# A two-block hybrid layer stack in split fp32 on one core: a third weight piece converted ahead, the gates' logarithms placed ahead of the attention steps, and query sums placed ahead of rotations

## The chip, the cores and the metric

One Trainium2 chip, of which one core runs the kernel. The time is device time of one execution in microseconds; the time stated is the median of several. The engines are called PE (TensorE, matmuls), PEld (its weight loads), ACT (ScalarE), DVE (VectorE), POOL (GpSimd) and SP (SyncE, which issues the DMAs). The granted clock is the share of full speed (2.4 GHz) that PE was given in a stretch.

## What is computed

A sequence of 16 meta and 512 other tokens of width 1024, in fp32, goes through two layers of a first block and two of a second. A layer of block 1 (`hybrid_layer`) is:

```python
h = rms_norm(x, norm_g);  z = h @ w_in
aq, ak, av, ag, mq, mk, mv, mi, mf, mo, mgate = jnp.split(z, split_points(), axis=-1)
q = apply_partial_rope(rms_norm(aq, q_norm_g), cos, sin)      # 16 heads of 64, 2 kv heads
k = apply_partial_rope(rms_norm(ak, k_norm_g), cos, sin)
ya = sliding_window_sink_attention(q, k, v, sink) * silu(ag)
mq, mk = split(silu(causal_depthwise_conv(concat[mq, mk])))
log_i = mi + b_i;  log_f = log_sigmoid(mf + b_f)              # the gates, one row per head
hm = mlstm_chunkwise(mq, mk, mv, log_i, log_f)
ym = rms_norm(hm) * sigmoid(mo) * silu(mgate)
return x + concat([ya, ym]) @ w_out
```

A layer of block 2 has a memory of keys and values, made by a projection of a normalised memory, differential attention in 32 steps, three groups of local attention, softmaxes over dilated units, gates, three branches and an output projection. All of it is again projections of the normalised input by slices of one wide weight matrix, with softmaxes and gates on the results.

## The kernel before, in words

**Weights.** All weights come as a stream of pieces of 128 x 1024 fp32 values (512 KB) in a fixed order. A step `("w", r)` turns piece r from the staging ring (2 buffers, `st`) into two halves: ACT copies it to a rounded high half `ch`, DVE subtracts that from the piece and gives the low half `cl`. Both have rings of 3 buffers (`NST, NCV = 2, 3`). The wait of ACT ahead of the copy is for the DMA of piece r and for the last matmul that read piece r-3. SP issues the DMA of piece r+2 once `cl` of piece r is done. Activations are kept as `hh` and `hl`, so each product takes three matmuls: hh x ch, hl x ch, hh x cl. A projection of one 128-wide tile over 8 slices of K and 2 token halves in block 1 is 48 matmuls; a unit of two tiles reads two pieces, and each piece serves both tiles with half of K.

**Order.** The class `Order` writes one list of steps by hand, and each engine executes its share of each step in the order of the list, with semaphore waits where a step needs the result of another engine. So what stands ahead of a step in the list stands ahead of it in the queue of every engine that both use. `Order.weights` puts the next `("w", r)`; `proj` and `projr` call it twice behind a unit's last tile, and in the places where a piece serves one tile alone (`lvpm`, `o1`, `br`, `o2`) it is called once for each piece. At the start of the list, `order()` puts the first two pieces at k = 4 and 6 of the loop over the input tiles. The evacuation of a projection (`cvev`, `qkev`, `agev`, `lvev`, `lgev`, `gtev`, `dqkev`) is put behind `proj`, so behind those conversions.

**Block 1, attention stage (`block1`).** 32 attention steps: `sA` (transposes, scores, maximum), `sB` (exponentials), `sC` (probabilities times values), for step s, s-1, s-2 in loop turn s, over head pairs; beside each, `fill(s)` puts projections by the table `SCHED1`: mv tiles (`mvmm`) in steps -3 to 1, conv tiles 0 and 1 at steps 2 and 3, query tiles 2 and 3 at steps 4 and 5, mv again at 6 to 10, and so on in turns of 8 steps; from 29 the attention gate's tiles (`ag`). Attention steps 8, 16 and 24 are the first to use query tiles 2, 4 and 6. For a query tile, `chain()` walks through three stages, one per loop turn: x = 0 `qsum` (sums of squares on PE, DVE scale, pow on POOL), x = 1 `rope` (scaled tile times cosine on POOL, shifted copy by DMA times sine and an addition on DVE), x = 2 `ropeq` (writes the `ZR` query operand on DVE). Query tiles come in pairs one step apart, so while the odd tile is at stage x, the even one is at x + 1; `st["turn"]` holds them in order of the tile.

**Gates in block 1.** `gra` takes bias, absolute value, exponential and logarithm on a 4 x 528 tile (ACT); the exponential and the logarithm are in different table sets, so it has two table loads. `grf` has 8 parts: 0 and 1 are additions, a fill and scans on DVE, the next ones smaller, part 7 writes and reads rows through DMAs. `grt` brings results to token order. In the kernel before `gra` is put at step 0 behind `sA`, `grf` parts 0 to 7 at steps 1 to 8 and `grt` at step 5.

**Block 2 (`block2`).** 35 steps of differential attention with projections beside them (`SCHED2`), `dnorm`, three local groups (`lq`, then values by `lvmm`/`lvpm` with `lvev`, then scores and softmax `lS`), the softmax over 3 parts (`lse0`, `lse1`, `lse2`) between projections `mq(0)` and `mq(1)`, 16 transposed dilated units (`eT`, `eP`) with the gates `lg` ahead and behind, the additions `yasp`, memory attention `fA`/`fB` with gate projections (`mg`, `gate`), branches `br` and the output `o2`.

In the profile all engine calls of a kind have one line, that of the helper: L92 matmul, L95 transpose, L98 activation, L101 tensor_tensor, L105 tensor_scalar, L109 scalar_tensor_tensor, L116 scan, L119 copy, L122 reduce.

Of the kernel before, what the change touches and what calls it, by code (L numbers as in the profile page):

```python
# [290 lines left out]
class Order:  # L291
# [6 lines left out]
    def put(self, *step):  # L298
        self.o.append(step)
# [90 lines left out]
    def block1(self, l, sums):  # L390
        put, nid = self.put, l
# [3 lines left out]
        def later():  # L395
            if st["conv"]:
                t, g = st["conv"]
                put("conv", l, t, g, self.nsq())
            st["conv"] = None

        def chain():

            todo, st["turn"] = st["turn"], []
            for t, n, x in todo:
                if t == 8 and x == 0:
                    put("qkn", l)
                    n = rot(t)
                else:
                    put(("qsum", "rope", "ropeq")[x], l, t, n)
                if x < (1 if t == 8 else 2):  # L410
                    st["turn"].append((t, n, x + 1))

        def rot(t):
            put("rot", l, t, self.rot)
            self.rot += 1
            return self.rot - 1

        def qk(t, u):
            self.proj(("q", l, t), nid, L, u, t % 2)
            chain()  # L420
            put("qkev", l, t)
            st["turn"].append((t, rot(t), 0))

        def fill(s):
            later()
            for kind, a, b in SCHED1[s]:
                if kind == "mv":
                    if b == 0:
                        st["u"] = self.unit(1, l, 3328 + 256 * a)
                    put("mvmm", l, a, b, st["u"])  # L430
                    if b == 4:
                        self.weights()
                        self.weights()
                    put("mvev", l, a, b)
                    continue
                later()
                if a % 2 == 0:
                    st["u"] = self.unit(1, l, {"cv": 2304, "ag": 1280, "q": 0}[kind] + 128 * a)
                if kind == "q":
                    qk(a, st["u"])  # L440
                    continue
                self.proj((kind, l, a), nid, L, st["u"], a % 2)
                if kind == "cv":
                    g = self.ng()
                    put("cvev", l, a, g)
                    st["conv"] = (a, g)
                else:
                    n = self.nsq()
                    put("agev", l, a, n, self.ng())
# [12 lines left out]
        g = self.ng()  # L462
        put("vev", l, g)
        chain()
        self.norms(nid, 3, 4)
        put("gr", l)
# [8 lines left out]
        put("mvones", l)  # L475
        for a in range(3):
            fill(a - 3)
            chain()
        for s in range(35):
            if s < 32:  # L480
                put("sA", l, s)
            if s == 0:
                put("gra", l)
            if 1 <= s < 9:
                put("grf", l, s - 1)
            if s == 5:
                put("grt", l)
            if not any(x[0] == "q" for x in SCHED1[s]):
                chain()
            fill(s)  # L490
            if 0 <= s - 1 < 32:
                put("sB", l, s - 1)
            if 0 <= s - 2 < 32:
                put("sC", l, s - 2)
            if s == 26:
                put("m_s", l)
            if s == 27:
                put("m_t", l)
            if s == 28:
                put("m_o", l)  # L500
            later()
# [297 lines left out]
def order():  # L799
    m = Order()  # L800
    m.put("load")
    m.put("lines")
    m.put("consts")
    add, flush = m.squares(0)
    for k in range(9):
        if k < 8:
            m.put("xt", k)
        if k:
            m.put("raw", 0, k - 1)
        if k in (4, 6):  # L810
            m.weights()

    def first(k):
        add(k)
        if k == 7:
            flush()
    sums = m.block1(0, first)
    m.block1(1, sums)
    for l in range(2):
        m.block2(l)  # L820
    assert m.taken == len(m.plan) == m.converted
    return m.o
def program(nc, I, out):
    with ExitStack() as ctx:
        sig = Signals()
        steps = order()

        def sb(name, cols, dt=F32, p=128):
# [2095 lines left out]
```

How the kernel before makes its waits and increments, by code:

```python
    def wait_ge(self, *keys):  # L77
        for k in keys:
            if self.e is None:
                self.sig.asked.add(k)
            elif self.sig.at[k] is not None:
                name, v = self.sig.at[k]
                if v > self.seen.get(name, 0):
                    self.e.wait_ge(self.sig.sem[name], v)
                    self.seen[name] = v
# [954 lines left out]
            def acquire(key, ring, apart=False):  # L1040
                n = turn_of.get(ring, 0)
                turn_of[ring] = n + 1
                banks = rings[ring][n % len(rings[ring])]
                for b in banks:
                    pe.wait_ge(*held[b])
                    held[b] = [("free", key, b - banks[0])] if apart else [("free", key)]
                held_by[key] = banks
# [6 lines left out]
            def xt(k):  # L1055
                acquire(("xt", k), "PA")
                ps = ps2(("xt", k))
                pe.wait_ge(("x",))
                for a in range(4):
                    pe.transpose(ps[:, 0, 128 * a:128 * a + 128], xs[:, a, 128 * k:128 * k + 128], idf)
                pe.transpose(ps[:, 1, 0:16], meta[:, 128 * k:128 * k + 128], cst[0:16, C_ID:C_ID + 16]).then_inc(
                    "pe_x", ("full", ("xt", k)))
# [1 line left out]
            def sqp(sid, k, n):  # L1064
# [2 lines left out]
                    acquire(key, "P3")  # L1067
                ps = ps2(key)
                pe.wait_ge(("sqa", sid, k), ("ones",))
                for j, (o, w) in enumerate([(0, HALF), (HALF, HALF)] if lo == 0 else [(0, 512)]):
```

## Time and profile before

| | us |
|---|---|
| median of 3 runs | 3089.79 |
| lowest to highest | 3086.59 to 3089.86 |
| profiled execution | 3090.76 |
| its span | 3088.9 |
| PE busy | 2958.4 |
| DVE busy | 1617.1 |
| ACT busy | 1264.7 |
| POOL busy | 181.9 |
| mean granted clock | 0.981 |

Busy is the time in which an engine has an instruction under way. The page also lists groups of instructions with the idle time of the engine just before them and what ended it; the timeline gives each instruction with its start and, in brackets, the idle time before it and the engine and tile whose result ended it. "x2" is two like instructions run together, and the duration is that of both.

### The profile page before, as it was taken

Reading aid. Unit: us, or ns where it says so; the run is one execution under the profiler, and the core shown is the slowest. Engines: PE = TensorE matmul, PEld = TensorE weight load, DVE = VectorE, ACT = ScalarE, POOL = GpSimd, SP = SyncE. Lnnn points to the kernel's source line nnn. Section 1 sums busy time; section 2 is a strip of 40 time slices with the busy share of each in tenths; the row PEclk is TensorE's granted clock in tenths of the full one; section 3 lists DMA queues with packets and bytes.
Section 4 is the critical chain, followed back from the end, with each engine's and each line's share of the span. In section 5 each row is a group of like instructions: output and inputs, shape, how many; then the busy total and the mean of one; then the engine's idle time right before and its main releaser. Section 6 shows DMA issues by size and latency. Waiting matters only on the chain.

```text
span 3088.9 us, 44910 instructions
## 1 busy us (share of the span) xinstructions
PE 2958.4 (96%) x18366; PEld 2582.2 (84%) x18366; DVE 1617.1 (52%) x3255; ACT 1264.7 (41%) x2640; POOL 181.9 (6%) x207
## 2 busy tenths in 40 slices
PE   8899999988999999999999999999999999999998
PEld 6799888987999889888888877887888888877886
DVE  5666645346675453677433564334677433554324
ACT  4455423244554232565424433223566334433222
POOL 2100000010000000100000000000100000000000
PEclk9899999998999999999999999999999999999999
DMA  3111321211113222322233222333322232222222
GB/s 102 55 44 58 105 67 62 86 48 44 57 57 105 67 80 85 113 86 68 82 110 96 69 82 69 96 96 96 113 87 68 82 117 89 81 70 76 95 96 82
DMA packets 99735, 250.24 MB, mean 81 GB/s; under 512 B 8597, under 2 KB 44845, under 8 KB 99274
## 3 DMA queue, kind: packets, MB, share of 16 engines
q1 hardware_dynamic: 99530, 247.37, 25.2%
q8 instruction: 145, 2.38, 0.3%
q14 instruction: 60, 0.49, 0.0%
HBM read 239.60 MB, written 6.50 MB: 80 GB/s over the span
## 4 chain that ended last, share of the span: by engine, by line
PE 81%; DVE 11%; ACT 4%; issue 1%; DMA 1%; POOL 1%; DVEq 0%; POOLq 0%; SPq 0%; ACTq 0%
PE ps L92 78%; PE ps L95 3%; ACT Z L98 2%; DVE cl L101 2%; DVE Z L101 2%; DVE Z L109 1%; DVE ZR L101 1%; DVE Z L119 1%; DMA st<-in_stream_dram 1%; DVE Z L105 1%; DVE stat L122 1%; ACT ch L98 1%; ACT L98 0%; POOL stat L101 0%; DVE sq L109 0%
## 5 line engine op out<-in xcount | busy, mean ns | idle before, releaser
L92 PE MATMUL ps<-hh,ch 128*128 128x264 f32 (+1 forms) x2688 | 824.6, 348 | 54.2 <-DVE cl L101 32.1
L92 PE MATMUL ps<-hl,ch 128*128 128x264 f32 (+1 forms) x2880 | 851.7, 340 | 0.0
L92 PE MATMUL ps<-hh,cl 128*128 128x264 f32 (+1 forms) x2688 | 811.7, 343 | 0.0
L101 DVE TENSOR_TENSOR cl<-st,ch 128x1024 fp32r<-128x1024 f32 (+1 forms) x436 | 495.8, 1152 | 531.3 <-ACT ch L98 531.1
L92 PEld LDWEIGHTS ps<-hh,ch 128*128 128x128 f32 x2688 | 468.4, 192 | 128.7 <-issue 27.4
L98 ACT ACTIVATE ch<-st 128x1024 fp32r<-128x1024 f32 (+1 forms) x436 | 424.8, 990 | 357.0 <-PE ps L92 328.3
L92 PEld LDWEIGHTS ps<-hl,ch 128*128 128x128 f32 x2880 | 500.1, 192 | 59.1
L92 PEld LDWEIGHTS ps<-hh,cl 128*128 128x128 f32 x2688 | 468.4, 191 | 58.9
L98 ACT ACTIVATE Z<-ps 128x512 f32<-128x512 f32 (+7 forms) x510 | 218.9, 438 | 600.3 <-PE ps L92 479.8
L92 PE MATMUL ps<-ZR,ch 128*128 128x264 f32 (+2 forms) x1728 | 426.5, 342 | 5.6 <-DVE cl L101 5.2
L92 PEld LDWEIGHTS ps<-ZR,ch 128*128 128x128 f32 x1728 | 289.1, 191 | 48.8 <-issue 12.9
L92 PE MATMUL ps<-Z 128*128 128x128 f32 (+11 forms) x1564 | 272.7, 318 | 25.2 <-DVE Z L119 15.1
L92 PEld LDWEIGHTS ps<-Z 128*128 128x128 f32 (+6 forms) x1564 | 205.8, 186 | 81.5 <-issue 47.3
L92 PE MATMUL ps<-ZR,cl 128*128 128x512 f32 (+2 forms) x704 | 223.7, 348 | 0.0
L92 PE MATMUL ps<-ch,hh 128*128 128x256 f32 (+2 forms) x736 | 214.2, 291 | 2.5 <-DVE cl L101 2.5
L92 PE MATMUL ps<-cl,hh 128*128 128x256 f32 (+2 forms) x736 | 211.2, 287 | 0.0
L92 PE MATMUL ps<-ch,hl 128*128 128x256 f32 (+2 forms) x736 | 210.7, 286 | 0.0
L98 ACT ACTIVATE Z<-Z,stat 128x512 f32<-128x512 f32 (+4 forms) x264 | 151.2, 587 | 121.3 <-DVE stat L105 112.4
L92 PE MATMUL ps<-ZR 128*128 128x256 f32 (+4 forms) x1040 | 179.0, 333 | 9.9 <-DVE stat L105 9.9
L95 PE MATMUL ps<-cst,Z 128*128 128x128 f32 (+3 forms) x974 | 151.0, 274 | 8.0 <-DVE Z L101 5.9
L119 DVE COPY Z<-ps 128x512 f32<-128x512 f32 (+7 forms) x132 | 70.5, 547 | 157.5 <-PE ps L92 115.6
L92 PEld LDWEIGHTS ps<-ZR 128*128 128x128 f32 (+2 forms) x1040 | 123.4, 191 | 29.8 <-DVE stat L105 11.3
(133 smaller groups left out, 3213.6 us busy)
## 6 DMA issues: line engine op xcount, KB each, us to landing
st<-in_stream_dram SPq DMA_DIRECT2D x372, 512.0 KB, 3.6
st<-in_stream_dram SPq DMA_DIRECT2D x64, 256.0 KB, 3.3
Z<-decay_rows SPq DMA_DIRECT2D x8, 904.0 KB, 6.4
Z<-bias_lines SPq DMA_DIRECT2D x16, 448.0 KB, 4.1
ya_spill<-Z SPq DMA_DIRECT2D x8, 512.0 KB, 4.5
Z<-ya_spill SPq DMA_DIRECT2D x2, 2048.0 KB, 7.7
Z<-in_x_dram SPq DMA_DIRECT2D x4, 512.0 KB, 5.6
Z<-in_mem_dram SPq DMA_DIRECT2D x2, 1024.0 KB, 6.1
```

Of the source, the lines that this page charges most:

```text
L92: return Ins(self, self.e and self.e.matmul(o, a, b, start=start, stop=stop, skip_group_check=True))
L95: return Ins(self, self.e and self.e.transpose(o, a, i))
L98: return Ins(self, self.e and self.e.activation(o, i, f, **kw))
L101: return Ins(self, self.e and self.e.tensor_tensor(o, a, b, op))
L105: return Ins(self, self.e and self.e.tensor_scalar(o, a, s1, s2, op0))
L109: return Ins(self, self.e and self.e.scalar_tensor_tensor(out=o, in0=a, scalar=s, in1=b, op0=op0, op1=op1))
L119: return Ins(self, self.e and self.e.tensor_copy(o, i))
L122: return Ins(self, self.e and self.e.tensor_reduce(o, i, X, op, negate=negate))
```

## The change

Three edits, all of them to the order of the steps: (1) at the start a third piece is converted ahead, so that each later conversion step converts the piece one further in the stream; (2) `gra` goes from step 0 to the prologue turn a = 0, ahead of `chain()`, `grf` parts 0 and 1 to a = 1 and 2, parts 2 to 7 to steps 1 to 6, and `grt` to step 3; (3) within `chain()` the tiles are taken in order of their stage instead of order of the tile, so the odd tile's sum comes ahead of the even tile's rotation, and the odd tile's rotation ahead of the even tile's `ropeq`.

```diff
@@ -401,7 +401,7 @@
         def chain():
 
             todo, st["turn"] = st["turn"], []
-            for t, n, x in todo:
+            for t, n, x in sorted(todo, key=lambda y: y[2]):
                 if t == 8 and x == 0:
                     put("qkn", l)
                     n = rot(t)
@@ -475,15 +475,17 @@
         put("mvones", l)
         for a in range(3):
             fill(a - 3)
+            if a == 0:
+                put("gra", l)
+            else:
+                put("grf", l, a - 1)
             chain()
         for s in range(35):
             if s < 32:
                 put("sA", l, s)
-            if s == 0:
-                put("gra", l)
-            if 1 <= s < 9:
-                put("grf", l, s - 1)
-            if s == 5:
+            if 1 <= s < 7:
+                put("grf", l, s + 1)
+            if s == 3:
                 put("grt", l)
             if not any(x[0] == "q" for x in SCHED1[s]):
                 chain()
@@ -807,7 +809,7 @@
             m.put("xt", k)
         if k:
             m.put("raw", 0, k - 1)
-        if k in (4, 6):
+        if k in (4, 6, 8):
             m.weights()
 
     def first(k):
```

## Rows read from the trace of the kernel before

**Rows 1.** the page: busy time of the engines, its share of the span, instructions

```profile
PE 2958.4 (96%) x18366; PEld 2582.2 (84%) x18366; DVE 1617.1 (52%) x3255; ACT 1264.7 (41%) x2640; POOL 181.9 (6%) x207
```

**Rows 2.** waits of PE: line, releaser: us in total, times, longest

```profile
PE ps L92 <- DVE cl L101: 45.2, 27, 6.9
```

**Rows 3.** timeline, PE, steps 2 to 7: start, us, instruction, [idle before <-releaser]

```profile
101.99 0.78 PE L92 MATMUL ps<-hh,ch 128*128 128x264 f32 x2 [6.86 <-DVE cl L101]
123.95 0.78 PE L92 MATMUL ps<-hh,ch 128*128 128x264 f32 x2 [3.64 <-DVE cl L101]
151.42 0.58 PE L92 MATMUL ps<-ZR 80*128 80x256 f32 x1 [2.41 <-DVE stat L105]
```

**Rows 4.** windows: stretch, length, busy per engine, PEclk, DMA share, GB/s

```profile
102.00:106.50 4.50, 4.50 (x20) 4.50 (x21) 3.16 (x10) 1.32 (x5) 0.00 (x0) 0.50 0.67 221
107.00:110.00 3.00, 3.00 (x27) 3.00 (x26) 2.04 (x3) 0.00 (x0) 0.00 (x0) 1.00 0.00 1
536.00:540.00 4.00, 3.28 (x15) 3.31 (x16) 3.66 (x8) 2.24 (x3) 0.00 (x0) 0.61 0.40 131
```

**Rows 5.** timeline, ACT, step 0 (`gra`)

```profile
89.84 0.72 ACT L98 ACTIVATE Z<-Z,par 4x528 f32<-4x528 f32 x1
90.59 1.32 ACT L98 ACTIVATE Z<-Z 4x528 f32<-4x528 f32 x2
91.93 1.28 ACT L98 ACT_TABLE_LOAD   x1
93.22 0.64 ACT L98 ACTIVATE Z<-Z 4x528 f32<-4x528 f32 x1
```

**Rows 6.** timeline, DVE, steps 1 and 2: scan and subtractions

```profile
99.48 1.25 DVE L116 TENSOR_TENSOR_SCAN Z<-Z 4x528 f32<-4x528 f32 x1
100.66 2.32 DVE L101 TENSOR_TENSOR cl<-st,ch 128x1024 fp32r<-128x1024 f32 x2
```

**Rows 7.** timeline, POOL, DVE and PE, steps 14 to 16: tiles 4 and 5

```profile
206.50 1.95 POOL L101 TENSOR_TENSOR stat<-stat,par 128x10 f32<-128x10 f32 x1 [51.83 <-ACT Z L98]
...
208.41 1.30 POOL L101 TENSOR_TENSOR Z<-Z,cst 128x528 f32<-128x528 f32 x1
...
216.59 1.04 DVE L109 SCALAR_TENSOR_TENSOR stat<-stat,par 128x1 f32<-128x1 f32 x2
...
220.70 0.71 DVE L101 TENSOR_TENSOR ZR<-Z,ZR 128x528 fp32r<-128x528 f32 x1
221.32 0.70 DVE L101 TENSOR_TENSOR rot<-rot,cst 128x528 f32<-128x528 f32 x1
...
221.51 0.28 PE L92 MATMUL ps<-mskb,idb 128*128 128x144 bf16 x2 [1.19 <-issue]
```

**Rows 8.** timeline, PE, start of the output projection of block 1

```profile
536.72 1.10 PE L92 MATMUL ps<-ZR,ch 128*128 128x264 f32 x4 [1.78 <-DVE cl L101]
```

**Rows 9.** timeline, PE, block 2: memory's k/v; start of layer 1

```profile
1252.15 0.39 PE L92 MATMUL ps<-ch,ZR 128*128 128x256 f32 x1 [1.78 <-DVE cl L101]
...
2199.73 0.47 PE L92 MATMUL ps<-hh,ch 128*128 128x512 f32 x1 [2.25 <-DVE cl L101]
```

**Rows 10.** timeline, local values of group 2 and scores behind them

```profile
1738.63 1.06 ACT L98 ACTIVATE ch<-st 128x1024 fp32r<-128x1024 f32 x1 [5.21 <-PE ps L92]
...
1739.73 1.23 DVE L101 TENSOR_TENSOR cl<-st,ch 128x1024 fp32r<-128x1024 f32 x1 [5.05 <-ACT ch L98]
...
1741.48 1.29 DVE L119 COPY Z<-ps 128x512 f32<-128x512 f32 x2 [0.53 <-PE ps L92]
...
1743.66 2.20 PE L92 MATMUL ps<-Z 128*128 128x128 f32 x16 [0.50 <-DVE stat L112]
```

**Rows 11.** timeline, `yasp` additions behind the second gate unit, and PE

```profile
1830.31 3.09 DVE L101 TENSOR_TENSOR ZR<-Z,ZR 128x512 fp32r<-128x512 f32 x5
...
1836.55 0.50 PE L92 MATMUL ps<-hh,ch 128*128 128x512 f32 x1 [1.43 <-ACT Z L98]
```

**Rows 12.** timeline, PE, behind gate tile (0,1)

```profile
1882.35 2.47 PE L92 MATMUL ps<-Z 128*128 128x128 f32 x10 [3.07 <-DVE Z L119]
```

## Prediction

> **What bounds the kernel now.** I read the page's table of engines first [rows 1]: TensorE (PE) is busy 2958.4 of a span of 3088.9 us, so 130 us is all that any reordering can give back, apart from the clock; VectorE, ScalarE and GpSimd have most of their time free. So this is a case of waits, not of work. The waits of PE come next [rows 2]: the largest single item is the low half of a converted weight piece (`cl`), 45.2 us in 27 waits. I then listed each matmul that had been waited for, in order of time. Two waits of each block-1 layer make up most of it, 6.86 and 3.64 us [rows 3], with twins 601 us later; both layers together 21.0 us. Their neighbours are a wait for statistics, 2.41 us, ahead of an attention step [rows 3]. What is left of the 45.2: 1.25 x2 at the k/v unit, 1.78 x2 in the output projection [rows 8], 0.32 x4, and so 16.9 us for block 2, of which [rows 9] are two of the three longest. What a wait costs beyond itself is in the windows [rows 4]: behind the 6.86 us idle, the granted clock is 0.50 (1.2 of 2.4 GHz) for 4.5 us and back at 1.00 after; half of full speed over 3.5 to 4.5 us is some 1.7 to 2.2 us of lost matmul time. The window behind the 1.78 us of the output projection shows 0.61. I count 1.7 us for a wait like these that appears or goes.
>
> **How the three edits work.** *Third piece.* A unit has two halves of weights; with three converted buffers the conversion put at a unit's end was that of the piece whose buffer the unit's first half had freed. Now the last one put is that of the piece whose buffer frees at the end of the unit's last matmul. Gain: the first piece of the next unit is ready a unit earlier, so most `cl` waits can go. Cost: ScalarE (ACT) stands in the conversion's wait until the projection ends, then converts for 1.06 us [rows 10]; the evacuation of that projection's PSUM, put behind it, starts 1.1 us later; VectorE (DVE) stands in its subtraction (1.16 us each, [rows 6]) until ACT is done, so what DVE does with the unit's result starts 2.3 us after the projection's end, and SyncE's issue of the next piece stands in the same line. Where the result isn't needed soon this is hidden by the matmuls behind it; where PE's next work needs it, it is paid. Bytes, matmuls and conversions stay the same in number.
>
> *Gates' logarithms.* In ACT's queue at step 0 lie 0.72 + 1.32 + 1.28 (table load) + 0.64 us [rows 5], and a second load of 1.28 before the next Exp, 5.2 us in all, ahead of the pieces' conversion; on DVE the scan's 1.25 us, and an addition and a fill before it, lie ahead of the two subtractions (2.32 us, ending at 102.98), and PE's 6.86 us end there, at 101.99 [rows 3, 6]. Moved to the three prologue steps, where PE has mv matmuls whose weights are there, this goes from the path. The load itself lasts 1.28 us and the rows on both sides touch it (90.59 + 1.32 = 91.91, load at 91.93, next row at 93.22), so two switches take 2.6 us. The Trainium skill, "ScalarE: Activation LUTs", section What ACT_TABLE_LOAD costs, puts a load with the drain before it at some 2.7 us, so two at 5.3: by the page the move would free 2.7 us more of ACT, and the trace does not agree, since no drain stands between the rows.
>
> *Query sums ahead of rotations.* Sorting by stage turns "rotate the even tile, sum the odd one" into the reverse, and one step later puts the odd tile's rotation ahead of the even tile's last step, which writes the ZR that the attention step sA(8, 16, 24) multiplies.
>
> **Block 1, per layer, term by term** (+ is time saved).
> Steps -3 to 8: the 6.86 us lose ACT's 5.2 us; the conversion is also a unit ahead, so the wait goes nearly whole, but sA(0) and the tiles behind it are then late by the gates' work placed in the prologue; followed through, PE's gain at the first conv unit is about 4. The 3.64 us end on a DVE that had the next part of the gates' scan, as long as the one in [rows 6] or more, ahead of two subtractions; they shrink, and then the chain sum, pow, rotation, last step of tiles 2 and 3 sets sA(8) as it does now (it is what the 2.41 us of [rows 3] and its neighbours belong to). I get sA(8) 4.1 us earlier, after a wait of its own of over 1 us that costs 1.7 of clock: +2.4. Bounds: the two waits whole with clock, 6.86 + 3.64 + 2 x 1.7 = +13.9; or the chain eats it all, 0 (not below: no ACT or DVE work is added there). I take 2.4 since the chain's steps are the same instructions as before on both engines.
> sA(16): now the last step for tile 4 ends at 220.70 + 0.71 and PE goes on at 221.51 after 1.19 us idle (the profile names "issue", but the start stands at the end of that DVE row) [rows 7]. Sorted, tile 5's add pair (0.70 + 0.71, starting at 221.32 before) lies ahead: 1.4 us; and tile 4's rotation itself waits for a pow of 1.95 us on GpSimd that was behind the 1.30 us product [rows 7], of which about 0.6 reaches the path: -2.0, and the longer idle, about 3.2 us, turns the clock down: -1.7. Sum -3.7. sA(24) the same with less to wait for: -1.8 - 1.7 = -3.5. Bounds of each: 0 (if the even rotation's neighbours free DVE earlier) to -5.
> On GpSimd beside DVE: the pair of small DVE operations at 216.59 lasts 1.04 us in [rows 7], while GpSimd runs its product. The Trainium skill, "SBUF — State Buffer", section Who interferes with whom, gives this for a DVE instruction with two SBUF inputs beside a GpSimd one that reads SBUF. By it the sort, which moves the pow up by a step, moves such a meeting rather than adding one: 0.7 us either way, no more than the bounds just named.
> The output projection's 1.78 us [rows 8] goes, with the slow clock behind it (0.61 in [rows 4]): +3.4. Bounds 0 and 3.4. The 0.32 x2: +0.6. The attention gate unit that closes the stage pays the late evacuation: -1.1 - 0.4 = -1.5 (bounds 0 and -2.8).
> Sum: 2.4 - 3.7 - 3.5 + 3.4 + 0.6 - 1.5 = -2.3, for two layers -4.6.
>
> **Block 2.** *Gains.* Of the 16.9 us of `cl` waits, those in the memory's k/v (the first row of [rows 9]) end on a DVE that does norms ahead of the subtraction: the lead saves a third, 1.1 + 1.5. The waits at the block's start (0.88 and, behind a late piece, 2.25, the second row of [rows 9]) and ahead of dnorm (1.18 x2) go; the one behind the second softmax piece goes but its subtraction then lies ahead of the softmax's normalisation, -0.5 net in one layer and 0 in the other; 0.4 x2 goes. Sum 2.6 + 3.1 + 2.4 - 0.5 + 0.8 = +8.4. Bounds: 0 and 16.9.
> *Losses, per layer.* Local values (lvpm, then lS): now the projection ends at 1741.38, DVE copies at 1741.48 (1.29 us), and PE has 16 matmuls of its own and waits 0.50 us for the scores [rows 10]. The conversion at 1738.63 waited for the other half's end, [5.21 <-PE]; the new one waits for 1741.38, 1.06 us of ACT and 1.23 us of DVE come ahead of the copy, so it starts at 1743.7 instead of 1741.5: -2.25. This is for groups 1 and 2; for group 0, where two subtractions lie near there already, -1.3: -5.8. First gate unit ahead of the exponentials' transposes: -1.8 (of 2.3, 0.5 is idle). Second: the five additions (3.09 us), the maximum and the exponentials behind them already make PE wait 1.43 us [rows 11], so all that is put ahead on DVE and ACT, 1.9 us, is paid. Gate tile (0,1): PE already waits 3.07 us for a copy behind three additions [rows 12]: two conversions lie ahead now and one more of them moves behind the end: -1.35. First attention step of a head pair, three times: -0.4 each, -1.2. Sum -12.05, for two layers -24. Bounds: half of it, if PE's matmuls in flight cover as in the other units, -12; or with the clock: four of these waits grow over 1 us, 8 x 1.7 = -13.6 more, -38. I take -24 without clock, since two of the four are over 1 us today and pay for the clock already.
>
> **Sum.** -4.6 + 8.4 - 24 = -20. The profiled execution took 3090.76 us, 1.0 above the median of 3089.8; on the median 3089.8 + 20 = 3110.
>
> **Rivals.**
> A. *The lead pays and the queueing is covered.* If PE has work everywhere behind a unit's end (it is 96% busy and matmuls are queued ahead), the block-2 losses are nothing and the sort costs little: +8.4, and block 1 +2.4 + 3.4 + 0.6 without the sort's 7.2, up to +13.9 in the first term: 2 x 6.4 to 2 x 17.9. Time 3089.8 - 8.4 - 12.8 = 3068.6, at the far end 3046. For it: 45.2 us are named by the profile. Against: [rows 10, 11, 12] show PE idle just behind a unit's end already. It decides if the copy after a local-values unit starts less than 0.5 us late.
> B. *Waits are exchanged.* Same edits, half of block 2's losses (-12), gains +8.4 and block 1 even: 3089.8 + 3.6 = 3093, within the noise of the rest.
> C. *Clock on top.* As forecast, with new idle of over 1 us behind local values and gates turning the clock down each time: 3110 + 13.6 = 3124. It decides if the new idle stretches are followed by a clock as that of [rows 4].
> D. *The third piece changes nothing.* The ring has three buffers and the wait for the buffer is the same instruction order; if no conversion starts earlier than now because the staging DMA behind it is late, only sort and gates act: -3.7 - 3.5 + 2.4 per layer, 3089.8 + 9.6 = 3099. Against: [5.21 <-PE] in [rows 10] shows the buffer, not the DMA, as the last thing waited for.
>
> **How the numbers follow.** Forecast 0.35, C 0.18, D 0.07, A 0.22, B 0.18. Likeliest 3110 (its own range 3099 to 3118). For 8 in 10 the range leaves out A's far half and C's end: 3068 to 3126. Less than 0.2% (6 us) can't be told from no change: faster 0.22 (A, the better edge of B), same 0.14 (most of B), slower 0.64 (forecast, C, D, the rest of B).
>
> **What would show it.** Right: behind a unit's last matmul in block 2 the ACT row is a conversion of 1.06 us that waited for PE, and the copy starts over 2 us after the projection's end; PE's waits for `cl` fall from 45.2 to under 20, those for DVE Z, stat and ACT Z grow by over 25; idle ahead of sA(16) is about 3 us; 6.86 is gone, the clock behind it 1.00; the output projection has no wait. Wrong: PE's idle at the local scores is still 0.5; sA(16) starts no later than its neighbour tiles before; or the prologue's steps show new waits of over 2 us (the gates' work ahead of sA(0)), which no term here contains.

## The result and the profile after

The changed kernel takes 3160.18 us (median of 4 runs, 3157.14 to 3164.36) against 3089.82 us of the kernel before in the same session: a ratio of 1.0238, interval 1.0225 to 1.0251. The medians are 70 us apart (the ratio gives 73). The direction was forecast; the size was not (+20), and the time lies above the range, which ended at 3126.

The page after, with the line that answers to [rows 1], and the chain of work that ended last:

```profile
span 3157.5 us, 45008 instructions
PE 2973.8 (94%) x18366; PEld 2592.1 (82%) x18366; DVE 1624.5 (51%) x3255; ACT 1264.9 (40%) x2640; POOL 184.8 (6%) x207
PE 77%; DVE 12%; ACT 5%; issue 3%; POOL 1%; DMA 1%; DVEq 0%; SPq 0%; POOLq 0%; ACTq 0%
```

The third line is the chain; before, it was PE 81%, DVE 11%, ACT 4%, issue 1%. The span grew by 68.6 us. The matmuls are the same in number (18366); PE is busy 15.4 us longer with them, which is the clock (mean 0.976, before 0.981), and so idle 53 us more. Split where block 2 begins, PE's busy time fell by 1.4 us ahead of it and grew by 16.8 us in it (1769.3 to 1786.1). The waits of PE (engine, line, releaser: us in total, times, longest), against the 45.2 us of [rows 2]:

```profile
PE ps L92 <- DVE ZR L101: 32.8, 14, 4.9
PE ps L92 <- ACT Z L98: 19.7, 12, 5.2
PE ps L92 <- DVE Z L109: 19.5, 15, 3.3
PE ps L92 <- DVE Z L119: 18.6, 16, 4.1
PE ps L92 <- DVE stat L112: 13.4, 8, 3.0
...
PE ps L92 <- DVE cl L101: 5.0, 5, 2.0
```

The waits for `cl` did what was forecast: 45.2 to 5.0 us. What took their place is larger: the query operand (ZR), evacuations by ACT (Z), gates' and branches' results (Z L109), local scores' statistics (L112). Where these lie is read by taking each matmul of the order in both traces and subtracting its start times (PE's order is the same but for ten small transposes of `grt` in each layer of block 1). The difference is -1.0 us when block 1 begins, +11.5 in its first layer's output projection, +24.1 in the second's, +48.6 at the end of block 2's first layer and +68.5 at the end. So block 1 lost 25 us (forecast 4.6) and block 2, with the end of block 1's last output projection, 44 (forecast 15.6).

The traced execution of the kernel before took 3090.76 us, and its medians in the sessions of the experiments are 3086 to 3088. So start times measured against it show a loss up to 5 us too small, a gain up to 5 us too large.

The attention step 16, which answers to [rows 7] (timeline; start, duration, instruction, idle before):

```profile
211.06 0.70 DVE L101 TENSOR_TENSOR rot<-rot,cst 128x528 f32<-128x528 f32 x1
211.23 2.34 POOL L101 TENSOR_TENSOR stat<-stat,par 128x10 f32<-128x10 f32 x1 [2.80 <-DVE stat L105]
213.54 2.60 POOL L101 TENSOR_TENSOR Z<-Z,cst 128x528 f32<-128x528 f32 x2
214.97 1.74 DVE L101 TENSOR_TENSOR Z<-Z,rot 128x528 f32<-128x528 f32 x1 [3.20 <-POOL Z L101]
216.63 0.68 DVE L101 TENSOR_TENSOR ZR<-ps,ZR 128x512 fp32r<-128x512 f32 x1
217.37 0.31 PE L95 MATMUL ps<-cst,ZR 128*80 128x128 f32 x1 [1.32 <-DVE ZR L101]
...
221.11 0.70 DVE L101 TENSOR_TENSOR rot<-rot,cst 128x528 f32<-128x528 f32 x1
221.85 0.71 DVE L101 TENSOR_TENSOR Z<-Z,rot 128x528 f32<-128x528 f32 x1
222.47 0.17 DVE L119 COPY Z<-Z 128x16 f32<-128x16 f32 x1
222.75 0.71 DVE L101 TENSOR_TENSOR ZR<-Z,ZR 128x528 fp32r<-128x528 f32 x1
223.56 0.28 PE L92 MATMUL ps<-mskb,idb 128*128 128x144 bf16 x2 [4.51 <-issue]
```

This is the sort at work. The odd tile's pow (2.34 us) now stands ahead of the even tile's cosine product on POOL, and DVE, which has begun that tile's rotation, stands 3.20 us for it with everything behind it: the operand made from PSUM (216.63), for which PE waits 1.32 us, the next softmax, tile 5's rotation, and last the operand of tile 4 (222.75), for which PE is idle 4.51 us instead of 1.19 (the profile says "issue", but PE starts 0.1 us behind the end of that DVE row). The addition itself takes 1.74 us with POOL's second product beside it. Before, it took 0.71:

```profile
213.39 0.71 DVE L101 TENSOR_TENSOR Z<-Z,rot 128x528 f32<-128x528 f32 x1
```

Windows behind two long idle stretches, one of 5.16 us ahead of 120.08 (for an evacuation) and this one of 4.51 us. The columns are stretch, length, busy of PE, PEld, DVE, ACT, POOL, clock, DMA share, GB/s:

```profile
120.10:124.50 4.40, 4.40 (x20) 4.40 (x21) 3.78 (x5) 1.92 (x6) 0.00 (x0) 0.50 0.66 232
223.60:228.00 4.40, 4.40 (x27) 4.15 (x28) 2.71 (x12) 1.64 (x6) 0.00 (x0) 0.61 0.00 0
```

Local values in block 2, which answer to [rows 10]:

```profile
1773.17 1.95 PE L92 MATMUL ps<-Z 128*128 128x128 f32 x16
1773.43 1.06 ACT L98 ACTIVATE ch<-st 128x1024 fp32r<-128x1024 f32 x1 [1.78 <-PE ps L92]
1774.39 1.07 ACT L98 ACTIVATE Z<-ps 128x512 f32<-128x512 f32 x2
1774.52 1.23 DVE L101 TENSOR_TENSOR cl<-st,ch 128x1024 fp32r<-128x1024 f32 x1 [1.61 <-ACT ch L98]
1775.66 1.28 DVE L119 COPY Z<-ps 128x512 f32<-128x512 f32 x2
...
1777.84 0.38 PE L92 MATMUL ps<-Z 128*128 128x128 f32 x1 [2.72 <-DVE stat L112]
```

As forecast, the conversion waits for the projection's end and DVE's copy starts 2.2 us later behind it; PE's idle went from 0.50 to 2.72.

### The profile page after: what moved, and what is told of

It is laid out like the page before. It is cut to its first block, busy times and chain, and to the rows that moved or that the text cites. A ratio compares the mean times of both kernels' runs of the same rounds, so it can differ in the third digit from the quotient of the medians.

```text
span 3157.5 us, 45008 instructions
## 1 busy us (share of the span) xinstructions
PE 2973.8 (94%) x18366; PEld 2592.1 (82%) x18366; DVE 1624.5 (51%) x3255; ACT 1264.9 (40%) x2640; POOL 184.8 (6%) x207
## 4 chain that ended last, share of the span: by engine, by line
PE 77%; DVE 12%; ACT 5%; issue 3%; POOL 1%; DMA 1%; DVEq 0%; SPq 0%; POOLq 0%; ACTq 0%
PE ps L92 74%; PE ps L95 3%; DVE cl L101 2%; ACT ch L98 2%; DVE Z L109 2%; ACT Z L98 2%; DVE Z L101 2%; DVE ZR L101 1%; DMA st<-in_stream_dram 1%; DVE Z L119 1%; POOL stat L101 1%; DVE Z L105 1%; DVE stat L122 0%; DVE sq L109 0%; ACT L98 0%
## 5 line engine op out<-in xcount | busy, mean ns | idle before, releaser
L92 PE MATMUL ps<-hh,ch 128*128 128x264 f32 (+1 forms) x2688 | 819.4, 346 | 42.6 <-ACT Z L98 13.6
L92 PE MATMUL ps<-Z 128*128 128x128 f32 (+11 forms) x1564 | 279.6, 323 | 44.8 <-DVE Z L119 16.8
L98 ACT ACTIVATE Z<-ps,stat 128x272 f32<-128x272 f32 (+2 forms) x160 | 84.1, 531 | 180.8 <-DVE stat L109 145.5
L95 PEld LDWEIGHTS ps<-cst,Z 128*128 128x128 f32 (+3 forms) x974 | 118.6, 145 | 35.0 <-DVE Z L101 7.2
```

What stands on the lines that cost most here:

```text
L92: return Ins(self, self.e and self.e.matmul(o, a, b, start=start, stop=stop, skip_group_check=True))
L95: return Ins(self, self.e and self.e.transpose(o, a, i))
L98: return Ins(self, self.e and self.e.activation(o, i, f, **kw))
```

## The experiments

Each kernel is the kernel before with the edit named. All ratios are to the kernel before in the same session (its medians were 3086.1, 3086.6 and 3088.3 us in the three). The last column is the difference of the medians; the ratios give up to 2 us more or less.

| kernel | edit | median us | ratio, interval | us against before |
|---|---|---|---|---|
| e1_piece | third piece | 3125.1 | 1.0123, 1.0108 to 1.0138 | +39 |
| e2_gates | gates moved | 3081.5 | 0.9980, 0.9971 to 0.9989 | -5 |
| e3_sort | sort | 3119.0 | 1.0102, 1.0086 to 1.0117 | +33 |
| e4_piece_gates | third piece, gates | 3118.0 | 1.0097, 1.0080 to 1.0114 | +32 |
| e5_late | third piece, converted late | 3069.2 | 0.9941, 0.9927 to 0.9956 | -17 |
| e6_qsum_first | half of the sort | 3110.5 | 1.0078, 1.0063 to 1.0093 | +24 |
| e7_rope_before_last | other half | 3097.8 | 1.0035, 1.0022 to 1.0048 | +11 |
| e8_gates_grt5 | gates, `grt` left at 5 | 3076.4 | 0.9966, 0.9954 to 0.9979 | -10 |
| e9_block1 | third piece in block 1 | 3080.5 | 0.9978, 0.9969 to 0.9988 | -8 |
| e11_pool_first | sort, POOL as before | 3099.6 | 1.0033, 1.0021 to 1.0044 | +11 |
| e12_change_late | change, piece late | 3112.2 | 1.0080, 1.0064 to 1.0097 | +24 |
| e13_late_gates5 | piece late, gates, `grt` at 5 | 3057.2 | 0.9903, 0.9888 to 0.9917 | -31 |

**Each edit alone.** e1:

```diff
-        if k in (4, 6):
+        if k in (4, 6, 8):
```

> Third piece alone. Theory Q (queueing behind the unit's end): block 2's whole loss of about 43 us belongs to this edit, in block 1 the waits for cl go (about 13 us over both layers) while evacuations behind the conversions cost some of it: 3089.8 + 35 = 3125, PE's waits for cl under 8 us. Rival S (the sort is the cause, the piece is free): about 3080 or less. Rival X (the edits are only bad together): within 6 us of 3090.

Measured +39, theory Q; PE's waits for `cl` are 7.1 us. By start times of the same matmuls e1 is 13.3 us ahead in block 1's last output projection and 33.6 behind at the end: 46.9 us lost from there on, 3.2 of them still in that projection.

e2 (the gates' hunks of the diff):

> Gates moved, alone. Theory Q: per layer the 6.86 us before the first conv unit shrink by the 4 us of ACT's gate work, and the attention step 0 starts some 3 to 4 us later behind the DVE part put into the prologue, so the sum is small: 3085 (3080 to 3092). Rival: the prologue's wait of 4.9 us seen in the changed kernel and its slow clock are paid in full while the conv unit still waits for the conversion: 3100.

Measured -5. The wait ahead of attention step 0 is 1.26 us here, not 4.9, so its large form needs the sort too; the first conv unit still waits 5.49 us for `cl`.

e3 (the `sorted` line):

> Sort alone. Theory Q+S: at each query pair DVE stands about 3.2 us for GpSimd's product behind the odd tile's pow, and the last step for the even tile comes behind the odd tile's rotation: about 4.5 us at sA(8), sA(16), sA(24) of each layer: 3089.8 + 27 = 3117. Rival (as my prediction had it, -3.6 each for two of the three): 3104. Rival (sort hidden, block 1's loss is from the piece's queueing): within 6 us of 3090.

Measured +33: more than theory Q+S, twice what my steps gave. The loss is all in block 1, about 15 us per layer.

e4:

> The change without the sort. Additive case: 3160 - 27 = 3133. If the sort's harm is only visible with the third piece (interplay), about 3140 or more; if sort and piece share the same idle time, above 3145.

Measured +32, nearly the sum of e1 and e2 (34). Against e4 the change is 38 to 43 us slower, by the way it is reckoned, while on the kernel before the sort costs 33: the difference appears only on top of the other edits. Subtracting e4's start times from those of the change shows it at four places of each layer, 4.9 us at sA(0), 7.1 at sA(8), 5.2 at sA(16), 6.3 at sA(24), less 2.6 behind the first. In e4 PE is idle 1.19 to 1.54 us at these four, in the change 4.51 to 4.86; in the kernel before the first conv unit's long wait swallows 2.0 us of sA(0)'s delay, which e3 shows and the change cannot. Which of the two other edits makes up how much of this was not run.

**The sort in halves.** e6 and e7 differ in one key:

```diff
-            for t, n, x in todo:
+            for t, n, x in sorted(todo, key=lambda y: (0, 2, 1)[y[2]]):
```

> Half of the sort: the odd tile's sum ahead of the even tile's rotation, but the even tile's last step still ahead of the odd tile's rotation. Theory P (GpSimd's product comes behind the pow, and DVE, in order, stands for it about 3.2 us): most of the sort's 33 us, 3109. Rival R (the odd rotation ahead of the even last step is the cause): within 6 us of 3088.

e7 has (1, 0, 1) in place of (0, 2, 1).

> The other half of the sort: the odd tile's rotation ahead of the even tile's last step, sums and rotations as before. Theory P: 1.4 us of DVE and what its clock costs at 3 attention steps per layer, 3088 + 6 x 2 = 3100 at most. Rival R: 3115 to 3121, the whole of the sort.

+24 and +11, together the sort's 33 and a little more: theory P, within 2 us of both of its figures. In e6 the same rows as in the change stand (pow 2.34, DVE idle 3.20, addition 1.75), and PE is idle 3.15 us ahead of sA(16) instead of 4.51: the difference is the odd rotation's 0.70 + 0.71.

**POOL's order alone.** e11 keeps the sort in all queues but POOL's:

```diff
             todo, st["turn"] = st["turn"], []
+            for t, n, x in todo:
+                if x == 1:
+                    put("ropep", l, t, n)
...
-load=load, rope=rope, qsum=qsum, vtr=vtr
+load=load, ropep=rope, qsum=qsum, vtr=vtr
```

> The whole sort, but GpSimd's product for a rotation is a step of its own that stands ahead of the sums, so GpSimd's queue is that of the kernel before, and the queues of DVE, PE, ACT and SP are those of the sorted kernel. Theory P (GpSimd's order makes the DVE stand 3.2 us): what is left is the other half of the sort, 3098 or less. Rival D (DVE's own order is the cause): 3119 as the sort alone.

+11 us, as e7 (3099.6 for "3098 or less", whose distance is within the interval). DVE's and PE's queues are those of e3, and 22 us are gone: the larger part of the sort's cost is one instruction order on an engine that is busy for 6% of the span. The 22 us hold both of its effects, DVE's 3.20 us of standing and the longer addition. In e11 the addition has POOL's pow beside it in place of a product, and it takes 0.71 us:

```profile
213.63 2.34 POOL L101 TENSOR_TENSOR stat<-stat,par 128x10 f32<-128x10 f32 x1 [3.18 <-DVE stat L105]
214.20 0.71 DVE L101 TENSOR_TENSOR Z<-Z,rot 128x528 f32<-128x528 f32 x1
```

**Where the conversion stands.** e5 keeps the lead of three pieces but owes the last conversion until the next projection step:

```diff
+    def put(self, *step):
+        if step[0] in self.USES:
+            self.pay()
+        self.o.append(step)
...
     def weights(self):
+        self.pay()
+        self.owed = 1
```

> Third piece ahead as in the change (no sort, gates as before), but the last conversion that a unit's end asks for is put just ahead of the next projection step in place of right behind the unit's last matmul, so the evacuation and what follows it stand ahead of it in the queues of ACT and DVE. Theory Q (the loss is the queueing ahead of the evacuation, not the lead): block 1 keeps its 13 us, block 2's loss goes and some of its waits for cl too: 3062 (3050 to 3072). Rival L (the loss comes with the lead itself: later staging DMAs, the ring fully in use): 3110 or more.

`USES` names the projection steps; `pay` puts the owed conversion. -17 us instead of +39: 56 us between two places in the queues, with the same number of pieces ahead in the list, the same ring and the same transfers. Rival L is out. The matmuls of block 2 keep the difference they enter with (-22.8 us near its start, -23.2 at the end): placed late, the third piece costs and gains nothing there, while block 1 gains. This does not show that the lead is worth nothing in block 2, since the late place gives most of it back: the waits for `cl` there are 16.9 us before, 4.7 in e1 and 13.1 in e5. Block 2's end of layer shows both placements. e1:

```profile
2120.26 1.06 ACT L98 ACTIVATE ch<-st 128x1024 fp32r<-128x1024 f32 x1 [7.70 <-PE ps L92]
2121.35 1.23 DVE L101 TENSOR_TENSOR cl<-st,ch 128x1024 fp32r<-128x1024 f32 x1 [7.20 <-ACT ch L98]
2122.49 0.68 DVE L109 SCALAR_TENSOR_TENSOR xT<-ps,xT 128x512 f32<-128x512 f32 x1
...
2123.21 0.63 ACT L98 ACTIVATE sq<-xT 128x512 f32<-128x512 f32 x1 [1.89 <-DVE xT L109]
...
2123.99 1.10 PE L92 MATMUL ps<-sq,ones 128*128 128x512 f32 x2 [2.42 <-ACT sq L98]
```

and e5, where the square comes first and PE does not wait:

```profile
2089.96 0.63 ACT L98 ACTIVATE sq<-xT 128x512 f32<-128x512 f32 x1 [7.49 <-DVE xT L109]
2090.49 1.04 ACT L98 ACTIVATE ch<-st 128x1024 fp32r<-128x1024 f32 x1
2090.73 1.10 PE L92 MATMUL ps<-sq,ones 128*128 128x512 f32 x2
```

e9 leaves out one conversion step at block 1's end:

```diff
             put("o1", l, n, p, 8, 16)
-            self.weights()
+            if l == 0 or n < 7:
+                self.weights()
```

> Third piece ahead in block 1 only; one conversion step is left out at its end, so block 2 runs with two again (gates and chain as before). Theory Q: block 1 keeps its 13 us, block 2 is as in the kernel before: 3086.5 - 13 = 3073. If the two layers of block 2 react to how block 1 ended: anything over 3080.

-8 us: Q's sign, not its size; 3080.5 stands at the bound of the other case. By start times it is 12.6 us ahead in block 1's last output projection, 9.7 near its end, where the same loss appears as at block 2's output projection, and 8.6 at the end. So block 2 hardly reacts; the missing part was lost ahead of it.

**The token-order step.** e8 is e2 with `s == 5` for `grt`:

> Gates moved as in the change, but the step that brings them to token order stays at step 5. If the 4.2 us (ACT Z) ahead of the first query projection in the gates-alone kernel come from ACT standing for DVE's stat in that step (3.16 us in the changed kernel), they go and the time falls by some 6 to 10 us against the gates alone: 3074. If that wait has another cause, 3081 as with step 3.

-10 instead of -5. In e2 the rows ahead of the first query projection are

```profile
119.31 0.55 DVE L101 TENSOR_TENSOR Z<-Z 4x384 f32<-4x384 f32 x1
119.79 0.24 DVE L119 COPY stat<-ps 16x8 f32<-16x8 f32 x2
120.07 0.31 ACT L98 ACTIVATE stat<-stat 16x4 f32<-16x4 f32 x2 [3.16 <-DVE stat L119]
120.28 1.99 ACT L98 ACTIVATE ch<-st 128x1024 fp32r<-128x1024 f32 x2
...
122.18 0.58 ACT L98 ACTIVATE Z<-ps 128x528 f32<-128x528 f32 x1
...
122.81 0.81 PE L92 MATMUL ps<-hh,ch 128*128 128x264 f32 x2 [4.21 <-ACT Z L98]
```

ACT stands 3.16 us for DVE, and two conversions and the conv evacuation stand behind it. In e8 this wait is gone and one of 3.18 us for `cl` is in its place, so half of the hoped for gain came.

**Put together.** e12 is the change with e5's edit:

> The change with all three edits, but with the last conversion of a unit's end put just ahead of the next projection step. If the piece's cost is the same queueing here as alone (56 us between the two placements): 3160 - 56 = 3104. If sort and gates hide or add part of it: 3110 or more, or 3095 or less.

-49 us against the change by the two ratios, where the pieces alone gave 56: the sort or the gates take part of what the late conversion frees; e12 does not separate them. e13 has e5's edit and e8's, and no sort:

> No sort; third piece with its conversion put late, gates moved with the token-order step left at step 5. Additive: 3086.6 - 17.5 - 10.2 = 3059. If both remove the same wait of the first conv and query projections: 3066.

3057.2 us, 0.9903: faster than both kernels, and a little better than additive (-31 against -28). Without the sort nothing is lost between piece and gates, which points to the sort in e12.

## Why the prediction was right or wrong, point by point

The direction and the mechanisms held. What failed are three terms of the sum: the losses behind a unit's end in block 2 (24 us, where e1 shows about 52), the clock there, which is part of those 52 (put at nothing, where PE is busy 16.6 us longer with the same matmuls), and the sort (7.2 us per layer, where e3 shows 15 and the change 21 on top of the other edits).

- **Waits for `cl` go: right.** 45.2 to 5.0 us.
- **Queueing behind a unit's end: mechanism right, sum short; this is the step that failed in block 2.** Forecast for block 2 was 24 us lost and 8.4 gained, 15.6 net; e1 shows 43.8 net (46.9 with the end of the projection ahead). Taken apart by start times, in both layers together, the losses are about 52 us. The terms that I had are some 33 of it against 24: local values and scores 14.9 (11.6), first gate unit with the transposed units behind it 9.1 (3.6), second gate unit and additions 6.5 (3.8), gate tile (0,1) 2.5 (2.7), first attention steps nothing (2.4). The rest are places with no term at all: the transposes behind the first local projections 5.9, and the output projection with the layer's end and the memory's start 12.5. I read the places where PE already waited, and in [rows 9 to 12] looked for more of the same; at these transposes and in the output projection PE waited for next to nothing before, so no row pointed to them, though the same two instructions come ahead of the same kind of evacuation.
- **Clock: left out of the likeliest case, wrongly.** I didn't count it in block 2, arguing that those waits already paid for it. PE is busy 16.6 us longer there in e1 (16.8 in the change) with the same matmuls; that is rival C's 13.6, and it came on top of the idle time. The first gate unit is the plainest case: PE's idle time ahead of the first product grows by 1.0 us (0.44 to 1.44), and the delay by 4.4, because the clock is 0.50 behind it in e1 and 1.00 in the kernel before. The same eight matmuls of a transposed unit, before and in e1:

```profile
1794.31 1.06 PE L92 MATMUL ps<-Z 128*128 128x128 f32 x8
1794.22 1.92 PE L92 MATMUL ps<-Z 128*128 128x128 f32 x8
```

- **Gains in block 2: right.** Forecast 8.4. In e1 the waits for `cl` there fall from 16.9 to 4.7 us, and at the places that I named the start times move ahead by 8.1 us net: memory's k/v and the block's start 2.6 (5.7), the entry to `dnorm` 2.8 (2.4), the softmax 1.4 (0.5 lost), the two small waits 1.3 (0.8). That the parts differ and the sum fits is in part luck.
- **Steps -3 to 8 of block 1: right number by luck.** I gave sA(8) 4.1 us earlier and +2.4 behind it; in the change it starts 3.8 us earlier (160.22 to 156.43), and 2.7 are left ahead of sA(16). But this is the sum of two larger things. Without the sort, e4 is 10.5 us ahead at sA(8): 1.6 from before block 1, 3.2 at the k/v unit, whose wait of 1.25 us I had listed and given no term, and 5.7 in these steps, since the chain had more slack than I gave it. Against that stand 4.9 us at sA(0) and, with its clock, 7.1 at sA(8), less 2.6 between, which the sort costs. I had written that the term can't fall below 0 because no ACT or DVE work is added there; the sort changes the order there too. The sign of being wrong that I named, a new wait of over 2 us in the prologue, came (4.86 us at sA(0)), and it is for the most part the sort's: e2 has 1.26, e4 1.54. The late `grt` wait (5.16 us in the change), which I followed only as work on DVE, is the term's other part.
- **Sort: right sign, a third of its size; this is the step that failed in block 1.** Forecast 7.2 us per layer at two places; e3 has 15, and on top of the other edits about 21. Two errors. I priced the pow ahead of the product at 0.6 us "on the path" where the rows show DVE standing for 3.20 us, and counted only the tile concerned, not what is behind it in DVE's queue. And I took sA(16) and sA(24) alone; sA(0) and sA(8) have the same order.
- **DVE beside GpSimd: wrong.** I said that the sort moves such a meeting and adds none. The addition went from 0.71 to 1.74 us at 214.97 while POOL's product for the next tile runs. The Trainium skill, "SBUF — State Buffer", section Who interferes with whom, says that a DVE instruction with two SBUF inputs contends with a GpSimd one that reads SBUF. The trace agrees, at a price of 1.03 us at six of the eight even tiles (at all eight in e3). At the other two, tile 0 of each layer, DVE's addition starts some 0.1 us ahead of POOL's product (80.30 against 80.38); it takes its 0.71 us and the product 1.83 instead of 1.32. Beside a pow no price is seen (e11). No run separates it from the 3.20 us.
- **Table loads: right.** In the prologue the load at 77.67 touches its neighbours (76.33 + 1.32, then 78.96), and no drain is seen. The gates' move was worth little alone (-5), more with `grt` left where it was (-10).
- **Output projection: mis-sized.** +3.4 forecast; the 1.78 us went with its slow clock, but waits of 0.90 and 0.77 us for ZR came just ahead: about +1.1. The attention gate unit at the end of the stage, 1.5 lost in the forecast, lost 4.0 and 1.4 in the two layers of e1.
- **Rivals.** **A** (cover behind a unit's end) fell with e1: the copy behind the local values starts 2.2 us later, where A needed under 0.5. **B** (half of the losses) and **D** (the piece changes nothing) fell with e1's +39. **C** had the right mechanism, on top of losses that were themselves too small.

## What to carry to other kernels

A conversion, copy or prefetch that waits for the end of the work in flight must not stand ahead of that work's evacuation: each in-order engine then delivers its result late, and what it gains where results are not needed soon can be kept by putting the same step a little later (56 us here; where the late place gives the lead back, it at least costs nothing). When an order is changed, read the queue of every engine that a step touches, the least busy one too, and count all that stands behind an instruction that will wait, at each place where the pattern recurs; places without a wait today are the ones that no row warns of. A new idle stretch is to be priced with the slow clock behind it (here 1.0 us of idle time became 4.4 us).

## What the runs showed that was not expected

- An engine busy for 6% of the span set 22 us by its order (e3 against e11).
- A DVE addition of two SBUF operands took 1.74 us when it began just behind a GpSimd product, 0.71 when it began just ahead of it, beside a pow, or alone.
- A third converted piece is worth 17 us when its conversion is put late, all of it ahead of block 2.
